# Final norm ahead of the last expert block, whose rows are normed and stored by index afterwards

## What is computed

```python
h = x + (gc * conv_out + gg * gla_out) @ w_out
h = h + hier_moe(rms_norm(h, norm_ffn), ...)     # 32 experts, each token goes to 2 of them
y_prompt, y_sample = rms_norm(h_prompt, norm_final), rms_norm(h_sample, norm_final)
def rms_norm(x, g): return x * rsqrt(mean(x * x, -1) + EPS) * g
```

## Time and profile before

| what | us |
|---|---|
| median of 3 runs (lowest, highest) | 1757.73 (1754.54, 1759.61) |
| the profiled execution: its own time | 1755.28 |
| the profiled execution: span from first to last instruction | 1753.6 |
| TensorE busy | 1671.7 (95%) |
| VectorE busy | 1249.8 (71%) |
| ScalarE busy | 920.2 (52%) |
| GpSimd busy | 222.5 (13%) |

### The profile page before, as it was taken

The page is one execution under the profiler, slowest core; times in us unless marked ns, Lnnn a source line. Parts: engine busy times, 40 slices in busy tenths (PEclk is TensorE's granted clock), DMA queues, the critical chain, the costliest instruction groups (busy, mean ns, idle before and its releaser), DMA issues.

```text
span 1753.6 us, 24797 instructions
## 1 busy us (share of the span) xinstructions
PE 1671.7 (95%) x8928; PEld 1471.5 (84%) x8928; DVE 1249.8 (71%) x2079; ACT 920.2 (52%) x1172; POOL 222.5 (13%) x260
## 2 busy tenths in 40 slices
PE   7999999999999999999999987999999999999991
PEld 6999987777999999879998876888888888888771
DVE  5234799986676667655464558998989898888873
ACT  6263121216433344325333336788888787777864
POOL 3100111000000000001001222311111111211110
PEclk9999999999999999999999998999999999999996
DMA  5401223222243222355343338999999999999965
GB/s 196 142 26 73 73 97 105 92 80 79 76 141 119 90 90 91 100 194 195 126 167 124 109 128 361 338 366 370 368 387 385 386 390 391 378 375 387 358 214 204
DMA packets 103439, 366.99 MB, mean 209 GB/s; under 512 B 14461, under 2 KB 57681, under 8 KB 89536
## 3 DMA queue, kind: packets, MB, share of 16 engines
q1 hardware_dynamic: 80448, 308.76, 47.3%
q0 software_dynamic: 22704, 57.12, 10.1%
q10 hardware_dynamic: 208, 0.08, 0.0%
HBM read 325.13 MB, written 61.22 MB: 220 GB/s over the span
## 4 chain that ended last, share of the span: by engine, by line
PE 67%; PEld 19%; DMA 5%; DVE 4%; issue 2%; ACT 1%; PEldq 1%; DVEq 0%; ACTq 0%; SPq 0%; POOLq 0%
PE bank L1005 64%; PEld bank L1005 19%; PE bank L1436 1%; DMA wraw_up<-in_w_expert_up 1%; DMA wraw_down<-in_w_expert_down 1%; PE bank L1460 1%; DVE fbuf L2586 1%; DVE wL_down L1965 1%; DVE wL_up L1965 1%; PE bank L1357 0%; DMA cw_raw<-in_w_conv_out 0%; DVE wL_gate L1965 0%; PE bank L1014 0%; DMA wo_in<-in_w_out 0%; DMA uo<-in_x_prompt 0%
## 5 line engine op out<-in xcount | busy, mean ns | idle before, releaser
L1965 DVE TENSOR_TENSOR wL_down<-wraw_down,wH_down 128x1024 fp32r<-128x1024 f32 x144 | 166.7, 1220 | 32.2 <-ACT wH_down L1534 31.9
L1965 DVE TENSOR_TENSOR wL_up<-wraw_up,wH_up 128x2048 fp32r<-128x2048 f32 x72 | 161.6, 2286 | 20.3 <-ACT wH_up L1534 20.3
L1965 DVE TENSOR_TENSOR wL_gate<-wraw_gate,wH_gate 128x2048 fp32r<-128x2048 f32 x72 | 161.8, 2288 | 13.8 <-ACT wH_gate L1534 13.5
L1534 ACT ACTIVATE wH_up<-wraw_up 128x2048 fp32r<-128x2048 f32 x72 | 134.0, 1910 | 63.7 <-DMA wraw_up<-in_w_expert_up 39.8
L2079 DVE SCALAR_TENSOR_TENSOR ybuf<-uo,gwork,ybuf 128x1024 f32<-128x1024 f32 x120 | 153.7, 1281 | 6.1 <-issue 6.1
L1534 ACT ACTIVATE wH_down<-wraw_down 128x1024 fp32r<-128x1024 f32 x144 | 140.4, 1053 | 11.6 <-DMA wraw_down<-in_w_expert_down 11.6
L1534 ACT ACTIVATE stage<-bank 128x512 f32<-128x512 f32 (+4 forms) x63 | 33.4, 545 | 198.3 <-PE bank L1005 191.0
L1534 ACT ACTIVATE wH_gate<-wraw_gate 128x2048 fp32r<-128x2048 f32 x72 | 134.5, 1934 | 1.7 <-DMA wraw_gate<-in_w_expert_gate 1.7
L1005 PE MATMUL bank<-nTH,gateH 128*128 128x352 f32 x384 | 132.1, 344 | 0.6 <-issue 0.6
L1005 PE MATMUL bank<-nTH,slabH 128*128 128x352 f32 x384 | 125.9, 328 | 2.4 <-DVE nTL L1965 1.8
L949 POOL DMA_INDIRECT h_scr<-ybuf,kdT x36 | 71.3, 1981 | 433.1 <-ACT ybuf L1534 397.6
(11 more groups left out here) (316 smaller groups left out, 4248.3 us busy)
## 6 DMA issues: line engine op xcount, KB each, us to landing
wraw_gate<-in_w_expert_gate SPq DMA_DIRECT2D x36, 2048.0 KB, 15.1
wraw_up<-in_w_expert_up SPq DMA_DIRECT2D x36, 2048.0 KB
wraw_down<-in_w_expert_down SPq DMA_DIRECT2D x36, 2048.0 KB
slab_raw<-in_w_in SPq DMA_DIRECT2D x7, 2048.0 KB, 8.4
gate_scr<-stage POOLq DMA_DIRECT2D x16, 528.0 KB, 3.5
vr_scr<-stage POOLq DMA_DIRECT2D x32, 256.0 KB, 2.3
gate_raw<-in_w_in SPq DMA_DIRECT2D x16, 512.0 KB, 9.3
vrbuf<-vr_scr SPq DMA_DIRECT2D x16, 512.0 KB, 7.3
```

The source lines that it names most:

```text
L1534: return act.activation(out, in_, func, **kw)
L1965: return dve.tensor_tensor(out, x, y, op)
```

## The change

The nine tiles are loaded, normed and stored once the last block but one has landed in `h_scr`. The last block is no longer added to `h_scr`. ScalarE takes its 128 weighted rows into `y_rows` in SBUF; GpSimd gathers the 128 rows of `h_scr` that they belong to into `last_h`, by the slots' token list; VectorE adds the two (after the sixth of the nine tiles), ScalarE and VectorE norm the sum as a tenth tile, and GpSimd stores it by two indirect DMAs, one into `y_prompt` and one into `y_sample`, each of which skips the rows of the other. They are issued when all nine plain stores have landed, since those have written the same rows without the last block's part. A second list of slots, `lst_smp` (the token less 1024, and a number past the end for prompt tokens), is made by VectorE when the lists of the further blocks are ready. The norm is made in place, so that the tiles take half the room.

The core of the diff:

```diff
-        fbuf = at("fbuf", O_A, [P, 2, NT, D])
+        fbuf = at("fbuf", O_A, [P, NCH, D])
...
-            def all_scattered(n):
-                scatter(n)
-                pool.wait_ge(y_scattered[n % 2], 16 * (n // 2 + 1))
+            def last_block(n):
+
+                pool.tensor_copy(last_tok, lst_tok[:, n:n + 1])
+                pool.tensor_copy(last_smp, lst_smp[:, n:n + 1])
+                pool.wait_ge(y_scattered[(n - 1) % 2], 16 * ((n - 1) // 2 + 1))
...
-            pool.sem_inc(moe_done, 1)
+            pool.drain().then_inc(moe_done, 1)
+            pool.indirect_dma_start(out=last_h, out_offset=None, in_=h_scr,
+                                    in_offset=bass.IndirectOffsetOnAxis(ap=last_tok, axis=0),
+                                    bounds_check=T - 1, oob_is_err=False).then_inc(more_rows, 16)
+            pool.wait_ge(f_made, NT + 1)
+            pool.wait_ge(f_out, 16 * NT)
+            for dst, idx, n in ((o["y_prompt"][0], last_tok, SEQ),
+                                (o["y_sample"].rearrange("b s d -> (b s) d"), last_smp, S_T)):
+                pool.indirect_dma_start(out=dst, out_offset=bass.IndirectOffsetOnAxis(ap=idx, axis=0),
+                                        in_=last_h, in_offset=None, bounds_check=n - 1, oob_is_err=False) \
+                    .then_inc(scattered, 16)
+            pool.wait_ge(scattered, 16 * (2 * NT + 2))
...
-                    take_y(n, b, i * 16)
+                    w = lst_w[:, n:n + 1] if isinstance(n, int) else lst_w[:, bass.ds(n, 1)]
+                    act.wait_ge(ed_done, n + 1)
+                    f(y_rows[:, 0:512], bk[5], ACT.Copy, scale=w)
+                    f(y_rows[:, 512:D], bk[6], ACT.Copy, scale=w).then_inc(last_made, 1)
...
+            def final_rms(x, sums, root):
+                r = x.shape[0]
+                f(fjunk[0:r, :], x, ACT.Square, accum_out=sums)
+                act.drain()
+                f(root, sums, ACT.Sqrt, scale=1.0 / D, bias=eps_t[0:r, :]).then_inc(rms_made, 1)
+
             f(rstd9[0], eps_t, ACT.Sqrt)
             for t in range(NT):
                 r = rows(t)
                 act.wait_ge(tile_loaded[t], 48)
-                f(fo[t][0:r, :], fh[t][0:r, :], ACT.Square, accum_out=ss9[t][0:r, :])
-                act.drain()
-                f(rstd9[t][0:r, :], ss9[t][0:r, :], ACT.Sqrt, scale=1.0 / D, bias=eps_t[0:r, :]).then_inc(rms_made, 1)
+                final_rms(fh[t][0:r, :], ss9[t][0:r, :], rstd9[t][0:r, :])
+            act.wait_ge(last_made, 2)
+            final_rms(last_h, ss[0], rstd[0])
...
+            dve.drain()
+            dve.tensor_copy(lst_f, lst_tok)
+            dve.drain()
+            dve.tensor_scalar(lst_far, lst_f, float(SEQ), float(NO_PAIR), ALU.is_lt, ALU.mult)
+            dve.drain()
+            dve.scalar_tensor_tensor(lst_smp, lst_f, float(-SEQ), lst_far, ALU.add, ALU.add)
             dve.drain().then_inc(lists_ready, 1)
...
             for t in range(NT):
...
+                if t == 6:
+                    dve.wait_ge(last_made, 1)
+                    dve.wait_ge(more_rows, 32)
+                    tt(last_h, y_rows, last_h, ALU.add).then_inc(last_made, 1)
+                final_norm(t, fh[t][0:rows(t), :], rstd9[t][0:rows(t), :])
+            final_norm(NT, last_h, rstd[0])
```

More of the change, by code:

```diff
@@ L200, in hybrid_layer @@
         hidTL = at("hidTL", O_Y + R16 // 2 + KB2, [P, FC, P], FR)
-        fbuf = at("fbuf", O_A, [P, 2, NT, D])
+        fbuf = at("fbuf", O_A, [P, NCH, D])
+        assert 4 * NCH * D <= O_B
         def flat(t):
@@ L372, in hybrid_layer @@
         f_out = sem("f_out")
+        last_made = sem("last_made")
         def rows(t):
@@ L420, in hybrid_layer @@
         lst_w = flat(kdT)[:, NBLK:2 * NBLK]
+        lst_smp = flat(kdT).bitcast(I32)[:, 3 * P:3 * P + NBLK]
+        lst_f, lst_far = flat(kdT)[:, 3 * P + NBLK:3 * P + 2 * NBLK], mtab[:, 0:NBLK]
         slot_hot = [flat(kdT)[:, P * (1 + k):P * (2 + k)] for k in range(2)]
@@ L440, in hybrid_layer @@
         cnt = small[:, 32:32 + NE]
-        fh = [fbuf[:, 0, t, :] for t in range(NT)]
-        fo = [fbuf[:, 1, t, :] for t in range(NT)]
+        fh = [fbuf[:, t, :] for t in range(NCH)] + [xg[1]]
+        last_h, y_rows, fjunk = xg[0], gs[:, 0:D], gs[:, D:2 * D]
+        last_tok, last_smp = small[:, 24:25].bitcast(I32), small[:, 25:26].bitcast(I32)
         nfin = mtab[:, :]
@@ L770, in _ @@
                 dst = o["y_prompt"][0, t * P:t * P + P, :] if t < NCH else o["y_sample"].rearrange("b s d -> (b s) d")
-                sp.dma_start(dst, fo[t][0:rows(t), :]).then_inc(f_out, 16)
+                sp.dma_start(dst, fh[t][0:rows(t), :]).then_inc(f_out, 16)
             sp.wait_ge(f_out, 16 * NT)
@@ L980, in pool_block @@
                 if n + 1 < NBLK:
-                    maybe(pool, n_more > n + 1 - NE, pool.nop, lambda: all_scattered(n))
+                    maybe(pool, n_more > n + 1 - NE, pool.nop, lambda: last_block(n))
                 else:
-                    all_scattered(n)
+                    last_block(n)
             def later_gather(n):
@@ L2580, in _, with final_norm @@
             dve.wait_ge(norm_row_loaded, 32)
-            for t in range(NT):
[L2582 to L2587, removed]
+            def final_norm(n, x, root):
+                r = x.shape[0]
+                dve.wait_ge(rms_made, 2 * NT + n + 1)
+                dve.reciprocal(root, root)
+                dve.drain()
+                dve.scalar_tensor_tensor(x, x, root, nfin[0:r, :], ALU.mult, ALU.mult).then_inc(f_made, 1)
+            for t in range(NT):
+                if t == 6:
[4 more added lines that the diff above has]
+            final_norm(NT, last_h, rstd[0])
 _INS = ["x_prompt", "x_sample", "state_conv", "state_gla", "norm_mix", "w_in", "b_gates", "w_gla_gate_up",
```

## The result

The changed kernel takes 1761.05 us (median of 19 runs, 1758.31 to 1765.99) against 1757.73 us (19 runs, 1754.41 to 1761.19) for the kernel before on the same chip. The ratio is 1.0018, with a 95% interval of 1.0011 to 1.0026: 3.2 us slower. The forecast was 2.0 us slower, which it counted as no change, as it does everything under 0.3%. The profiled execution took 1758.71 us, its span is 1757.1.

What follows compares the result with a forecast made beforehand. The end was taken as bound by 8.65 MB through the DMA engines after `moe_done`. 1749.6 + 5.4 + 0.6 = 1755.6 us against a span of 1753.6, 2.0 us slower; median 1759.7, range 1753 to 1767.

Steps and rivals of the forecast that it cites:

- Landing of the last block but one: Scatter of the last block but one, now the one waited for: taken to land at about 1714.8 us.
- Walk through the branches: GpSimd's pass through its remaining branches after that landing: still 2.5 us, ending at 1717.3 us.
- The drain: New GpSimd drain ahead of `moe_done`: 7.8 us, 107 DMAs at 0.073 us, priced from the drains of lines 89 and 905.
- Start of the loads: First load of the nine tiles, behind the new drain: at 1725.1 us, 4.0 us earlier than now.
- ScalarE: ScalarE ready to norm at about 1725.1 us, waiting as now for the first tile, which lands at 1728.7.
- From the first load to the last plain landing: Nine tiles' stretch: 0.4 us more for the gather, the addition hidden in full DMA queues, last plain store landed at 1749.6.
- The two output scatters: Indirect stores behind the last plain landing: 0.8 + 1.05 + 0.3 + 3.3 = 5.4 us, between 4.6 and 9.
- The second list: VectorE's three instructions and three drains ahead of `hidTL`: under 1 us, hidden by 4.5 us of slack.
- The first: Rival, 20%: the drain ahead of `moe_done` is short, loads start at 1717.3, 3.5 us faster, median 1754.2.
- The second: Rival, 12%: every drain behind indirect DMAs is long, so the end drain stands open, 9.7 us slower, 1767.4.
- The third: Rival, 5%: drain ahead of `moe_done` short, end drain long, 3.5 us faster plus 7.7 slower, 1761.9.
- the fourth: Rival, 8%: output scatters wait longer or a code-fetch stall hits GpSimd's tail, up to 1765, or 1 to 2 us gained.

Runs made afterwards that it cites:

- e3: The kernel before with the increment of `moe_done` put on a GpSimd drain, nothing else changed: 1766.21 us, ratio 1.0038 to the kernel before.
- e1: The changed kernel with the drain ahead of `moe_done` replaced by a wait for the two slot copies: 1758.92 us, ratio 1.0008 to the kernel before.
- e2: The changed kernel with one more GpSimd drain, behind its scatter of block 27, where it is idle: 1753.51 us, ratio 0.9968 to the kernel before.
- e7: The changed kernel with one more GpSimd drain behind the scatter of block 11, 43 DMAs ahead of the drain before `moe_done`: 1756.42 us, one run.
- e10: e2 without the two indirect output stores and the wait for them: 1746.61 us, ratio 0.9941 to the kernel before.
- e4: The changed kernel with two 512-byte GpSimd stores of single numbers after each of 28 scatters, 56 DMAs more: 1961.91 us, ratio 1.1159 to the kernel before.
- e8: The changed kernel with 15 more GpSimd stores of 64 KB spread over the first 28 blocks, 122 DMAs: 1762.14 us, one run.
- e9: The changed kernel with 30 more GpSimd stores of 64 KB spread over 28 blocks, 137 DMAs: 1764.75 us, one run.
- e12: The changed kernel with 56 more GpSimd stores of 64 KB spread over 28 blocks, 163 DMAs: 1759.57 us, one run.
- e11: e2 without the drain ahead of `moe_done`, gather and `moe_done` issued at the landing, addition before the first tile: 1751.98 us, ratio 0.9968 to the kernel before.

## Why the prediction came out as it did

The forecast of no change over 0.3% and its main step held: the 11.8 us by which the landing comes earlier are eaten by a drain charged for 107 DMAs, and what is left doesn't pay for two scatters at the end. By its own steps:

- **Landing of the last block but one.** 1714.8 forecast, 1714.74 measured. Right.
- **Walk through the branches.** 2.5 us forecast, 3.36 measured. One gap in it is 1.03 us, where a branch otherwise takes 0.15; in e3, before the same drain, the walk was 2.5. The gap is there too in e1, which has no drain behind the walk, and in e2, e7 and e10; it is absent in e4, e8, e9 and e12, which have a few more instructions ahead of it. So the drain doesn't make it. What the gap is stays open.
- **The drain.** 7.8 forecast, 7.83 measured. Right, because the row of line 89, with 108 DMAs, was so near: e1 and e3 measure 8.07 for 110 and 7.91 for 108. As a rule for any number it was luckier than it looked. It fails above 110, and 107 lay just below; at 43 it would say 3.1 where 3.57 was measured. And its second support, the equal price at line 905, was a coincidence. That drain begins with a load still in flight and ends 1.3 to 1.4 us after its landing in all fourteen traces, while its end lies 6.9 to 7.8 us behind GpSimd's last instruction, for the same 99 DMAs. The shortest of them is that of e3, the drain and then the landing of its load, against 8689 ns and 7.5 us before:

```profile
L905 POOLq DRAIN  x1: 8155/8155/8155, 807.5 to 807.5; - x1
```
```profile
DMA to landing us min/median/max: 6.9/6.9/6.9
```

  Two drains of the kernel before that the forecast did not weigh say the same:

```profile
L789 POOLq DRAIN  x1: 6332/6332/6332, 2.5 to 2.5; - x1
```
```profile
L825 POOLq DRAIN  x1: 5285/5285/5285, 20.6 to 20.6; - x1
```

  The first has one DMA ahead of it and ends 0.1 us after that one has landed (2.33 + 6.4 us); the second has two and ends at most 0.6 us after the later one. So two things go into a drain of GpSimd in these traces, the landing of what is in flight and the DMAs issued; ahead of `moe_done` everything has landed, and the second is left.

  The Trainium skill, PSUM — Partial Sum Buffer, section Engine vs sequencer instructions, has a drain wait for the engine to be idle. GpSimd was idle for 4.4 us when this one began, so that rule doesn't cover its 7.83 us; e2 and e3 show what that costs.
- **Start of the loads.** 1725.1 forecast, 1725.95 measured. The difference is the walk.
- **ScalarE.** Forecast to be ready at 1725.1 and to wait for the first tile as before; it was ready at 1725.95 and waited 3.73 us. Right.
- **From the first load to the last plain landing.** Before 1753.2 - 1729.14 = 24.1 us, forecast 0.4 more, measured 1751.59 - 1725.95 = 25.6. **This is the mis-sized term.** The last store is issued 20.4 us after the first load instead of 18.3, and lands in 5.2 instead of 5.8. The addition (1.22 us at 1740.88) was costed at nothing "in full DMA queues", but the last store could be issued only after it, and the queue behind was not deep enough to swallow a delay of 2.1 us. The other 0.9 us fits the 0.81 that ScalarE waited for the third tile (VectorE then starts its third scaling 0.74 us late). That the addition costs its 1.2 us was shown only in e11 against e2, where VectorE sets the pace; how much of it counts in the changed kernel itself was not tried.
- **The two output scatters.** 5.4 us forecast and 0.6 for the end: 6.0. Measured from 1751.59 to 1757.1: 5.5 (0.9, then 1.03, 0.30, 2.7 from the second's start to its landing, and 0.6). e10 agrees with 4.7, within some 4 us by the ratios, and with 4.8 by the end stretches. The landing was 0.6 us quicker than the fastest gather that it was taken from.
- **The second list.** Under 1 us forecast, hidden. VectorE's timeline:

```profile
1124.76 0.15 DVE L2589 COPY kdT<-bank 128x16 f32<-128x16 f32 x1
1124.98 0.19 DVE L2591 CAST kdT<-kdT 128x48 f32<-128x48 int32 x1
1125.25 0.46 DVE L2593 TENSOR_SCALAR mtab<-kdT 128x48 f32<-128x48 f32 x1
1125.79 0.21 DVE L2595 SCALAR_TENSOR_TENSOR kdT<-kdT,mtab 128x48 int32<-128x48 f32 x1
1126.11 0.69 DVE L1992 TENSOR_TENSOR hidTL<-bank,hidTH 128x512 fp32r<-128x512 f32 x1
```

  From the copy to `hidTL` it is 1.35 us, 1.1 more than before (1123.94 - 1123.67 = 0.27), and TensorE reads `hidTL` at 1130.29, 3.5 us behind its end. Right.

The sum over the forecast's span of 1755.6: +0.85 for the walk, +1.15 for the stretch of tiles, -0.5 for the end: 1757.1.

**The rivals.** The first (a short drain in the middle) had the wrong mechanism: e1 removes the drain and gains almost nothing. Its price was right for the case that nobody owes anything: it gave 3.5 us faster, and e2, which pays early, is 5.6 us faster by its ratio (3.7 to 7.7). The second (every drain behind indirect DMAs is long) fell with the 294 ns of line 89. The third's order, nothing charged in the middle and all of it at the end, appears in e1, for the reason of the forecast; its price was 4.2 us slower, and 1.4 was measured. Of the fourth nothing came in the new tail, which took 5.5 us of the 6.0 forecast; whether the 0.86 us of the walk are a stall in fetching code, of which it spoke, no run shows.

## What to carry to other kernels

A drain of GpSimd is charged for the DMAs that the engine has issued since its last one, here 0.07 to 0.09 us each for 11 to 110 of them, whoever waits behind it, and less for the higher numbers tried; so signal with a semaphore on the instruction that is waited for, and put one drain where the engine is idle, after most of the DMAs, since the one at the program's end falls due as soon as GpSimd is the last to finish. Work moved ahead of a wait gains only down to the next late thing: list every engine's readiness, and count the price of the fix-up that must now follow at the end (here 4.7 us for two indirect stores). Small work in a stretch where full DMA queues seem to hide all isn't free if the last store is issued behind it.

## What the runs showed of the hardware that was not expected

- With everything landed, a GpSimd drain grows with the DMAs since the last drain up to 110 (8.07 us) and is smaller above (4.60 at 122, 5.30 at 137, 2.2 at 163), for stores of 4 bytes a row as for stores of 64 KB.
- With a load in flight, the drain of line 905 (910 or 911 in the changed kernels) ends 1.3 to 1.4 us after its landing in all fourteen traces, whatever the landing took (6.9 to 7.8 us).
- 56 stores of 128 numbers of 4 bytes each cost 200 us; with 56 of 64 KB each no such cost shows (1759.57 us in one run, against 1761.05).
- A GpSimd addition of 128x1024 takes 3.37 us and stretches VectorE's three-operand scaling beside it from 1.28 to 3.14. The Trainium skill, SBUF — State Buffer, section Who interferes with whom, says that a VectorE instruction with two inputs in SBUF contends with a GpSimd one that reads SBUF; the rows agree.
- The records of the two GpSimd copies of one column, made beside VectorE's work on the weights, last 1.59 and 2.30 us and overlap, 2.7 us from start to end in the changed kernel.
